# Second layer's gate and up projections from an h normalised ahead, in 512-column matmuls; first layer's feed-forward activations moved by 32 bytes

## The chip, the cores and the metric

The kernel runs on one core of one Trainium2 chip. The metric is the time of one execution in microseconds, as the median of several runs. The core has TensorE (matmuls, with a separate weight load), VectorE (DVE), ScalarE (ACT), GpSimd (POOL) and SyncE (SP), which here issues the DMAs of the weights. The engines run side by side and wait for each other by semaphores.

## What is computed

Two layers of a diffusion backbone over 512 latent tokens (`x`) and 256 context tokens (`ctx`), width 1024. Each layer has a mixing half (windowed attention and a convolution group, one output projection) and a feed-forward half. The change is in the latter:

```python
D_MODEL = 1024; SEQ = 512; CTX_LEN = 256; DEPTH = 2; D_FF = 2816
def rmsnorm(x, g):
    y = xf * lax.rsqrt(jnp.mean(xf * xf, axis=-1, keepdims=True) + EPS)
    return y * g
def modulate(h, shift, scale):
    return h * (1 + scale) + shift
def swiglu(h, w_gu, w_dn):
    gu = h @ w_gu
    return (jax.nn.silu(gu[..., :D_FF]) * gu[..., D_FF:]) @ w_dn
...
h2 = modulate(rmsnorm(x, g_ffn[l]), sh2, sc2)
x = x + gt2 * swiglu(h2, w_gate_up[l], w_down[l])
if not last:      # the same for the context tokens, with their own shift, scale and gate
    ...
return rmsnorm(x, g_final)
```

In the second layer (index 1) no context token goes through the feed-forward half.

## The kernel before

Features lie on the 128 partitions, tokens along the free axis: `x` is [128, 8, 768], eight feature tiles of 512 latent and 256 context tokens. All weights are float32. To keep float32 accuracy each operand is split into a high part (rounded to float32r) and a low part (the rest), and a product is three matmuls: high x high, low x high, high x low (`tile_product`, L488; the matmul is L496). A weight block is 128 output features by eight k-tiles of 128 rows: SyncE loads it into `raw0` or `raw1` (L397), ScalarE writes `w_high` (`split_high`, L736) and VectorE `w_low` (`split_low`, L1015). Two blocks make a pair, one for each of the two slots: weights, PSUM banks (slot 0 has banks 0 and 1, slot 1 has 2 and 3) and `tmp` are double. ScalarE starts the copy for the next use of a slot when the block on it has ended, so its starts mark the ends of blocks.

The modulated norm is not applied before the matmul. What TensorE reads as `h_high` and `h_low` (`hH`, `hL`) is x times gain only. 1/rms is per token and is multiplied in afterwards, and the shift goes through the weights as two further columns (one for latent, one for context tokens), kept behind the tokens in the same rows: 512 + 2 + 256 + 2 columns, 3088 bytes. So a block's columns come in two groups, `mod_cols` (L281): with context 512 and 258, without it 256 and 258, since a bank holds 512 columns. Each group is a matmul of its own:

```python
def mod_cols(context):
    return [(0, 0, N), (1, HC, HW)] if context else [(0, 0, N // 2), (1, N // 2, HC)]
```

The feed-forward half goes in three chunks of 8, 8 and 6 tiles of D_FF: `gu0`, `dn0`, `gu1`, `dn1`, `gu2`, `dn2`. A gate/up phase has one pair for each tile of D_FF: slot 0 is the gate, slot 1 the up half. For each (`gu_pair`), VectorE copies the two shift columns (L1059) and multiplies the product by 1/rms into `tmp` (L1060), which frees the PSUM slot; ScalarE takes Silu of the gate with the shift as bias (L958); VectorE adds the shift to the up half and multiplies (L1385); ScalarE writes `ff_high` (`aH`, L964), VectorE `ff_low` (`aL`, L1389). VectorE handles all this in the written order: scaling of slot 0, `w_low` of slot 0, scaling of slot 1, `w_low` of slot 1, product, `ff_low`. The down phase has four pairs (eight tiles of x); its k-tiles are the chunk's tiles of D_FF, with one matmul of 512 columns and, in layer 0, one of 256. TensorE waits for `ff_low` tile by tile.

1/rms of layer 1's feed-forward norm (`rs`) is ready only while TensorE is in pair 0 of `gu0`, as its sums go over TensorE in between (`stat_tokens`, `stat_broadcast`).

In layer 0 VectorE also sums the modulation vectors of layer 1 (`ada_multiply`) between feed-forward blocks.

Places in SBUF are worked out by nested scopes; tiles of different stages share bytes. `ff_high` starts at a multiple of 128 bytes, its rows are 3072 bytes.

Of the kernel before, what the change touches and what calls it, by code (L numbers as in the profile page):

```python
# [27 lines left out]
P = 128  # L28
# [63 lines left out]


def key_columns(tokens, tiles):


    if tiles == (0, 1, 4, 5):
        return tokens.rearrange("p (a c) -> p a c", c=2 * P)[:, 0:3:2, :]
    step = tiles[1] - tiles[0]
    if step == 1:  # L100
        return tokens[:, P * tiles[0]:P * (tiles[-1] + 1)]
    return tokens.rearrange("p (t c) -> p t c", c=P)[:, tiles[0]:tiles[-1] + 1:step, :]
# [22 lines left out]
def hybrid_backbone(nc, xT, params, w_ada, w_conv, w_mix, w_out, w_gu, w_dn0, w_dn1, w_dn2,  # L125
                    rope, ident_in, masks_in, out):
    with ExitStack() as ctx:
        def sb(name, shape, dt=F32):
            return ctx.enter_context(nc.sbuf_tensor(name, shape, dt))

        def sem(name):
            return ctx.enter_context(nc.semaphore(name))
# [4 lines left out]
        wH = [sb(f"w_high{j}", [P, DT, P], F32R) for j in range(2)]  # L137
        wL = [sb(f"w_low{j}", [P, DT, P], F32R) for j in range(2)]
        ada_raw = sb("ada_raw", [P, AGW])
        wD = sb("w_conv", [P, 2, TG, P])  # L140
# [38 lines left out]
        with ExitStack() as h_scope:  # L179
# [22 lines left out]
            with ExitStack() as s:  # L202
                s.enter_context(nc.sbuf_tensor("gap_ff", [P, 2 * max(CHUNKS) * T], F32))
                ada_in_ff = s.enter_context(nc.sbuf_tensor("ada_in_ff", [P, AGW], F32))
            with ExitStack() as s:
                aH = s.enter_context(nc.sbuf_tensor("ff_high", [P, max(CHUNKS), T], F32R))
                aL = s.enter_context(nc.sbuf_tensor("ff_low", [P, max(CHUNKS), T], F32R))
        with ExitStack() as s:
            prob = s.enter_context(nc.sbuf_tensor("prob", [P, 3, 5 * P], F32))
            V = s.enter_context(nc.sbuf_tensor("v_tokens", [P, TB, KV * HD], F32))  # L210

            s.enter_context(nc.sbuf_tensor("gap", [P, CT * HW - 5 * P * 3 - TB * KV * HD], F32))
            aT = s.enter_context(nc.sbuf_tensor("attn_out", [P, CT, T], F32))
            s.enter_context(nc.sbuf_tensor("gap2", [P, CT * (HW - T)], F32))
            PT = s.enter_context(nc.sbuf_tensor("probT", [P, 2, 5, GRP, P], F32))
# [48 lines left out]
        ff_high, ff_low = sem("ff_high_ready"), sem("ff_low_ready")  # L264
        y_ok = sem("out_tile_ready")
        dve_self, pool_self = sem("dve_self"), sem("pool_self")

# [5 lines left out]
        def streams(context):  # L273
            return [(0, N, 0)] + ([(N, T, 1)] if context else [])
# [18 lines left out]
        def gains(layer, which, context, k):  # L293
            return [(a, b, gain[:, layer, which, k, v:v + 1]) for a, b, v in streams(context)]

        def shift_cols(slot):
# [127 lines left out]
        def _(pe):  # L424
# [86 lines left out]
            def conv_tile(layer, k):  # L511
# [16 lines left out]
                last.then_inc(conv_mm, 1)  # L528

            def phase(layer, name, ktiles, rhsH, rhsL, cols, ready=None, key=None, blocks=TB):  # L530

# [158 lines left out]
            for layer in range(DEPTH):  # L690
# [26 lines left out]
                for c, tiles in enumerate(CHUNKS):  # L717
                    phase(layer, f"gu{c}", DT, hH, hL, mod_cols(context), (h_ok, h_index[layer, "n2"]) if c == 0 else None,
                          (layer, "n2") if c == 0 else None, blocks)
                    phase(layer, f"dn{c}", tiles, aH, aL, tok_cols(context, False), (ff_low, layer * FT + sum(CHUNKS[:c])))  # L720
            stat_tokens((DEPTH, "n1"), NB)
# [4 lines left out]
        def _(act):  # L726
# [141 lines left out]
            for layer in range(DEPTH):  # L868
# [81 lines left out]
                for c, tiles in enumerate(CHUNKS):  # L950
# [3 lines left out]
                    def gu_pair(i, first=False):  # L954
# [8 lines left out]
                        act.wait_ge(ff_ok, i + (ff + 1))  # L963
                        f(aH[:, i, 0:width], tmp[1][:, 0:width], ACT.Copy).then_inc(ff_high, 1)  # L964

                    gu_pair(0, first=True)
                    with act.Fori(1, tiles - 1) as i:
                        gu_pair(i)
                    gu_pair(tiles - 1)

# [33 lines left out]
        def _(dve):  # L1004
# [246 lines left out]
            for layer in range(DEPTH):  # L1251
# [116 lines left out]
                for c, tiles in enumerate(CHUNKS):  # L1368
                    gu, dn = f"gu{c}", f"dn{c}"
                    ff = layer * FT + sum(CHUNKS[:c])  # L1370

                    def gu_pair(i):
                        dve.wait_ge(gemm, i * 2 + (2 * USES[layer, gu] + 1))
                        scale_product(0, context)
                        split_low(layer, gu, i, 0)
                        if isinstance(i, int):
                            for u in ada_units(layer, gu, 2 * i):
                                ada_multiply(u)
# [9 lines left out]
                        dve.wait_ge(ff_high, i + (ff + 1))  # L1388
                        tt(aL[:, i, 0:width], tmp[1][:, 0:width], f32(aH[:, i, 0:width]), ALU.subtract).then_inc(ff_low, 1)  # L1389
                        dve.wait_ge(ff_low, i + (ff + 1))  # L1390

                    apart = tiles - 1 if (layer, gu) in ADA_IN else 1
                    for i in range(apart):
                        gu_pair(i)
                        if i == 0 and (layer, gu) in SUM_IN:
                            ada_columns(SUM_IN[layer, gu])
                    if apart < tiles - 1:
                        with dve.Fori(apart, tiles - 1) as i:
                            gu_pair(i)
                    gu_pair(tiles - 1)  # L1400

# [224 lines left out]
```

## Time and profile before

| | |
|---|---|
| median of 3 runs | 1590.11 us (1589.21 to 1590.46) |
| profiled execution, its own time | 1588.25 us |
| its span | 1586.4 us |
| TensorE busy | 1533.7 us (97%), 9714 matmuls |
| VectorE busy | 936.5 us (59%) |
| ScalarE busy | 536.9 us (34%) |
| chain that ended last | TensorE 86%, VectorE 6%, ScalarE 4% |
| granted TensorE clock, mean | 0.99 of 2.4 GHz |

The span runs from the first to the last recorded instruction. In timelines each row has a start and a length in microseconds from the span's start, engine, line of the kernel, operation, and in brackets the idle time before it with what ended it. A matmul's length holds its passage through the array, which overlaps the next, so the pace of matmuls is read from start to start. The chain is followed back from the last instruction.

### The profile page before, as it was taken

Reading aid. Unit: us, or ns where it says so; the run is one execution under the profiler, and the core shown is the slowest. Engines: PE = TensorE matmul, PEld = TensorE weight load, DVE = VectorE, ACT = ScalarE, POOL = GpSimd, SP = SyncE. Lnnn points to the kernel's source line nnn. Section 1 sums busy time; section 2 is a strip of 40 time slices with the busy share of each in tenths; the row PEclk is TensorE's granted clock in tenths of the full one; section 3 lists DMA queues with packets and bytes.
Section 4 is the critical chain, followed back from the end, with each engine's and each line's share of the span. In section 5 each row is a group of like instructions: output and inputs, shape, how many; then the busy total and the mean of one; then the engine's idle time right before and its main releaser. Section 6 shows DMA issues by size and latency. Waiting matters only on the chain.

```text
span 1586.4 us, 24584 instructions
## 1 busy us (share of the span) xinstructions
PE 1533.7 (97%) x9714; PEld 1274.5 (80%) x9714; DVE 936.5 (59%) x1571; ACT 536.9 (34%) x858; POOL 128.4 (8%) x163
## 2 busy tenths in 40 slices
PE   6999998999999999999999999998999999999996
PEld 3865764688888888888888888676679998998995
DVE  2584689767666325765654466678786443443445
ACT  3312378724222112221122243148844222322222
POOL 0033221040000000000000001511020000000000
PEclk9999999999999999999999999999999999999998
DMA  9582600012333223333522123410022332323222
GB/s 358 207 242 58 241 12 27 1 54 107 119 122 103 67 81 144 119 115 123 191 74 62 54 70 108 137 54 1 28 67 93 93 93 93 93 93 95 93 87 83
DMA packets 39865, 161.16 MB, mean 102 GB/s; under 512 B 5616, under 2 KB 6000, under 8 KB 33648
## 3 DMA queue, kind: packets, MB, share of 16 engines
q1 hardware_dynamic: 35856, 148.72, 27.6%
q0 software_dynamic: 3936, 11.45, 2.6%
q8 instruction: 47, 0.77, 0.2%
q14 instruction: 26, 0.21, 0.0%
HBM read 149.76 MB, written 2.10 MB: 96 GB/s over the span
## 4 chain that ended last, share of the span: by engine, by line
PE 86%; DVE 6%; ACT 4%; issue 2%; POOL 1%; DMA 1%; SPq 0%; DVEq 0%; ACTq 0%; POOLq 0%
PE banks L496 74%; PE banks L525 3%; PE banks L613 2%; PE banks L433 1%; PE banks L640 1%; PE banks L625 1%; POOL z_padded L1528 1%; DVE row_max L1132 1%; PE banks L677 1%; PE banks L465 1%; ACT prob L819 1%; PE banks L483 1%; ACT w_high L736 1%; DMA ada_first<-in_w_ada 1%; ACT probT L831 1%
## 5 line engine op out<-in xcount | busy, mean ns | idle before, releaser
L496 PE MATMUL banks<-h_high,w_high 128*128 128x512 f32 (+1 forms) x1856 | 433.0, 314 | 3.9 <-DVE w_low L1015 2.4
L496 PE MATMUL banks<-h_high,w_low 128*128 128x512 f32 (+1 forms) x1856 | 427.8, 312 | 0.0
L496 PE MATMUL banks<-h_low,w_high 128*128 128x512 f32 (+1 forms) x1856 | 426.5, 311 | 0.0
L736 ACT ACTIVATE w_high<-raw 128x1024 fp32r<-128x1024 f32 (+1 forms) x178 | 185.3, 1041 | 697.0 <-PE banks L496 677.7
L496 PEld LDWEIGHTS banks<-h_high,w_high 128*128 128x128 f32 x1856 | 288.0, 189 | 38.3 <-issue 14.6
L1015 DVE TENSOR_TENSOR w_low<-raw,w_high 128x1024 fp32r<-128x1024 f32 (+1 forms) x178 | 216.3, 1215 | 171.1 <-ACT w_high L736 167.5
L496 PEld LDWEIGHTS banks<-h_low,w_high 128*128 128x128 f32 x1856 | 287.7, 189 | 21.1
L496 PEld LDWEIGHTS banks<-h_high,w_low 128*128 128x128 f32 x1856 | 286.4, 189 | 20.6
L1059 DVE COPY shift_product<-banks 128x2 f32<-128x2 f32 x116 | 18.4, 159 | 310.1 <-PE banks L496 299.2
L496 PE MATMUL banks<-ff_high,w_high 128*128 128x512 f32 (+1 forms) x528 | 160.5, 358 | 0.6 <-DVE ff_low L1389 0.6
L496 PE MATMUL banks<-ff_high,w_low 128*128 128x512 f32 (+1 forms) x528 | 159.6, 357 | 0.0
L496 PE MATMUL banks<-ff_low,w_high 128*128 128x512 f32 (+1 forms) x528 | 159.0, 355 | 0.0
L496 PEld LDWEIGHTS banks<-ff_high,w_high 128*128 128x128 f32 x528 | 87.1, 188 | 17.5 <-issue 1.7
L496 PEld LDWEIGHTS banks<-ff_low,w_high 128*128 128x128 f32 x528 | 87.1, 188 | 15.4
L496 PEld LDWEIGHTS banks<-ff_high,w_low 128*128 128x128 f32 x528 | 86.6, 188 | 14.9
L1060 DVE TENSOR_TENSOR tmp<-banks,inv_root 128x768 f32<-128x768 f32 (+1 forms) x116 | 94.9, 819 | 0.0
L1132 DVE TENSOR_REDUCE row_max<-banks 128x1 f32<-128x512 f32 (+2 forms) x80 | 55.0, 688 | 19.6 <-PE banks L613 19.1
L1108 DVE SCALAR_TENSOR_TENSOR x<-banks,mod,x 128x512 f32<-128x512 f32 (+1 forms) x96 | 60.3, 656 | 10.5 <-PE banks L496 10.5
L964 ACT ACTIVATE ff_high<-tmp 128x768 f32 (+3 forms) x44 | 32.5, 740 | 97.3 <-DVE tmp L1385 97.3
L613 PE MATMUL banks<-k_stacked,q_stacked 128*128 128x384 f32 (+2 forms) x224 | 59.2, 369 | 5.4 <-ACT esink L821 2.9
L1389 DVE TENSOR_TENSOR ff_low<-tmp,ff_high 128x768 fp32r<-128x768 f32 (+3 forms) x44 | 36.3, 825 | 41.0 <-ACT ff_high L964 41.0
L1271 DVE SCALAR_TENSOR_TENSOR conv<-z_padded,par,conv 128x512 f32<-128x512 f32 x90 | 57.0, 660 | 2.0
(171 smaller groups left out, 1623.5 us busy)
## 6 DMA issues: line engine op xcount, KB each, us to landing
raw<-in_w_gu SPq DMA_DIRECT2D x88, 512.0 KB, 3.5
ada_raw<-in_w_ada SPq DMA_DIRECT2D x21, 1024.0 KB, 5.7
raw<-in_w_dn SPq DMA_DIRECT2D x32, 512.0 KB, 3.5
raw<-in_w_mix SPq DMA_DIRECT2D x28, 512.0 KB, 5.0
ada_in_ff<-in_w_ada SPq DMA_DIRECT2D x12, 1024.0 KB, 5.5
raw<-in_w_out SPq DMA_DIRECT2D x16, 512.0 KB, 3.5
ada_first<-in_w_ada SPq DMA_DIRECT2D x7, 1024.0 KB, 14.1
raw<-in_w_dn SPq DMA_DIRECT2D x16, 384.0 KB, 3.0
```

The source lines that it names most:

```text
L496: last = mm(bank[:, 2 * slot + bk, 0:b - a], weights[w][:, k0_w + k, :], rhs[:, k0_rhs + k, a:b], start=(k == 0 and n == 0), stop=(k == kt ...
L525: last = mm(bank[QC * q:QC * q + QC, BC + bk, 0:b - a], wD[:, j, g, QC * q:QC * q + QC], zr[j][:, q, SH * g + a:SH * g + b], start=(g == 0 ...
L613: last = mm(wide[:, at:at + w], lhs, rhs, start=in_bank[m] not in in_bank[:m], stop=in_bank[m] not in in_bank[m + 1:], skip_group_check=True)
L736: f(wH[j][:, 0:k, :], raw[j][:, 0:k, :], ACT.Copy).then_inc(w_high, 1)
L964: f(aH[:, i, 0:width], tmp[1][:, 0:width], ACT.Copy).then_inc(ff_high, 1)
L1015: tt(wL[j][:, 0:k, :], raw[j][:, 0:k, :], f32(wH[j][:, 0:k, :]), ALU.subtract).then_inc(w_low, 1)
L1059: nc.vector.tensor_copy(shifted[:, slot, :], shift_cols(slot))
L1060: tt(like(tmp[slot]), src, like(rs), ALU.mult).then_inc(slot_free[slot], 1)
L1108: last = stt(out=xt, in0=bank[:, 2 * slot + (a >= N), 0:b - a], scalar=mod[:, layer, bass.ds(t + gate * DT, 1), v], in1=xt, op0=ALU.mult, ...
L1132: nc.vector.reduce_max(mx[:, c:c + 1], score_place(u, qs[q][2]), AX.X).then_inc(row_ok, 1)
L1271: made = stt(out=acc, in0=zt, scalar=col("w_dw", j, layer), in1=acc, op0=ALU.mult, op1=ALU.add)
L1389: tt(aL[:, i, 0:width], tmp[1][:, 0:width], f32(aH[:, i, 0:width]), ALU.subtract).then_inc(ff_low, 1)
```

## The change

Layer 0's gate/up is computed as before. In layer 1, pairs 0 to 2 of chunk 0 are too (`PLAIN = 3`). Meanwhile VectorE multiplies x by gain and 1/rms (`h_normal`, a ring of six tiles), ScalarE adds the shift and rounds (`h_normal_high`), and VectorE writes the rest (`h_normal_low`): three tiles after pair 0, three after pair 1, two after pair 2, the low parts of a group following inside the next pair, those of the last two after pair 2. From pair 3 of chunk 0 on, and in chunks 1 and 2, TensorE reads these with one matmul of 512 columns for each product; Silu and the product read PSUM directly. Layer 1's activations get tiles of their own with rows of 512 tokens (`lastH`, `lastL`); layer 0's start 32 bytes further (`gap_line`).

```diff
...
+PLAIN = 3
+HN_RING = 6
...
+        with ExitStack() as s:
+            hn_high = s.enter_context(nc.sbuf_tensor("h_normal_high", [P, DT, N], F32R))
...
-                s.enter_context(nc.sbuf_tensor("gap_ff", [P, 2 * max(CHUNKS) * T], F32))
+                s.enter_context(nc.sbuf_tensor("gap_ff", [P, 2 * max(CHUNKS) * T + 16], F32))
+                s.enter_context(nc.sbuf_tensor("gap_line", [P, 8], F32))
+            with ExitStack() as s:
+                lastH = s.enter_context(nc.sbuf_tensor("ff_last_high", [P, max(CHUNKS), N], F32R))
+                lastL = s.enter_context(nc.sbuf_tensor("ff_last_low", [P, max(CHUNKS), N], F32R))
+                hn_low = s.enter_context(nc.sbuf_tensor("h_normal_low", [P, DT, N], F32R))
+                hn = s.enter_context(nc.sbuf_tensor("h_normal", [P, HN_RING, N], F32))
+            ffH, ffL = (aH, lastH), (aL, lastL)
...
+        hn_scaled, hn_hi, hn_ok = sem("h_normal_product"), sem("h_normal_high_ready"), sem("h_normal_ready")
...
+        def normal_from(layer, c):
+            return DT if layer == 0 else PLAIN if c == 0 else 0
...
+            def last_gu(c):
+                layer, name = 1, f"gu{c}"
+                key = (layer, "n2")
+                plain = normal_from(layer, c)
+                for i in range(plain):
+                    for j in range(2):
+                        after = [(7, lambda: stat_tokens(key, NB))] if i + j == 0 else \
+                            [(2, lambda: stat_broadcast(key, NB))] if i == 0 else ()
+                        gemm_block(layer, name, i, j, DT, hH, hL, mod_cols(False),
+                                   (h_ok, h_index[key]) if i + j == 0 else None, after)
+                for j in range(2):
+                    gemm_block(layer, name, plain, j, DT, hn_high, hn_low, [(0, 0, N)],
+                               (hn_ok, 0) if plain and j == 0 else None)
+                with pe.Fori(plain + 1, PAIRS_OF[name]) as i:
+                    for j in range(2):
+                        gemm_block(layer, name, i, j, DT, hn_high, hn_low, [(0, 0, N)])
...
-                    phase(layer, f"gu{c}", DT, hH, hL, mod_cols(context), (h_ok, h_index[layer, "n2"]) if c == 0 else None,
-                          (layer, "n2") if c == 0 else None, blocks)
-                    phase(layer, f"dn{c}", tiles, aH, aL, tok_cols(context, False), (ff_low, layer * FT + sum(CHUNKS[:c])))
+                    if layer:
+                        last_gu(c)
+                    else:
+                        phase(layer, f"gu{c}", DT, hH, hL, mod_cols(context), (h_ok, h_index[layer, "n2"]) if c == 0 else None,
+                              (layer, "n2") if c == 0 else None, blocks)
+                    phase(layer, f"dn{c}", tiles, ffH[layer], ffL[layer], tok_cols(context, False),
+                          (ff_low, layer * FT + sum(CHUNKS[:c])))
...
-                        f(aH[:, i, 0:width], tmp[1][:, 0:width], ACT.Copy).then_inc(ff_high, 1)
-                    gu_pair(0, first=True)
-                    with act.Fori(1, tiles - 1) as i:
-                        gu_pair(i)
-                    gu_pair(tiles - 1)
+                        f(ffH[layer][:, i, 0:width], tmp[1][:, 0:width], ACT.Copy).then_inc(ff_high, 1)
+                    def normal_high(first, last):
+                        for k in range(first, last):
+                            act.wait_ge(hn_scaled, k + 1)
+                            f(hn_high[:, k, :], hn[:, k % HN_RING, :], ACT.Identity,
+                              bias=mod[:, layer, 3 * DT + k, 0:1]).then_inc(hn_hi, 1)
+                    def gu_normal(i):
+                        split_high(layer, gu, i, 0)
+                        f(act_out[:, 0:N], bank[:, 0, 0:N], ACT.Silu).then_inc(slot_free[0], 1)
+                        split_high(layer, gu, i, 1)
+                        act.wait_ge(slot_free[1], i + (USES[layer, gu] + 1))
+                        f(ffH[layer][:, i, 0:N], tmp[1][:, 0:N], ACT.Copy).then_inc(ff_high, 1)
+                    if layer == 0:
+                        gu_pair(0, first=True)
+                        with act.Fori(1, tiles - 1) as i:
+                            gu_pair(i)
+                        gu_pair(tiles - 1)
+                    else:
+                        plain = normal_from(layer, c)
+                        for i in range(plain):
+                            gu_pair(i)
+                            normal_high(*((0, 3), (3, 6), (6, 8))[i])
+                        with act.Fori(plain, tiles - 1) as i:
+                            gu_normal(i)
+                        gu_normal(tiles - 1)
...
-                    def gu_pair(i):
+                    def gu_pair(i, between=None):
+                        if between is not None:
+                            between()
...
-                        tt(aL[:, i, 0:width], tmp[1][:, 0:width], f32(aH[:, i, 0:width]), ALU.subtract).then_inc(ff_low, 1)
+                        tt(ffL[layer][:, i, 0:width], tmp[1][:, 0:width], f32(ffH[layer][:, i, 0:width]), ALU.subtract)\
+                            .then_inc(ff_low, 1)
-                    apart = tiles - 1 if (layer, gu) in ADA_IN else 1
+                    def normal_product(first, last):
+                        for k in range(first, last):
+                            if k >= HN_RING:
+                                dve.wait_ge(hn_ok, k - HN_RING + 1)
+                            stt(out=hn[:, k % HN_RING, :], in0=x[:, k, 0:N], scalar=gain[:, layer, 1, k, 0:1],
+                                in1=rs[:, 0:N], op0=ALU.mult, op1=ALU.mult).then_inc(hn_scaled, 1)
+                    def normal_low(first, last):
+                        for k in range(first, last):
+                            dve.wait_ge(hn_hi, k + 1)
+                            stt(out=hn_low[:, k, :], in0=hn[:, k % HN_RING, :], scalar=mod[:, layer, 3 * DT + k, 0:1],
+                                in1=f32(hn_high[:, k, :]), op0=ALU.add, op1=ALU.subtract).then_inc(hn_ok, 1)
+                    def gu_normal(i):
+                        split_low(layer, gu, i, 0)
+                        dve.wait_ge(gemm, i * 2 + (2 * USES[layer, gu] + 2))
+                        dve.wait_ge(slot_free[0], i + (USES[layer, gu] + 1))
+                        tt(tmp[1][:, 0:N], bank[:, 2, 0:N], act_out[:, 0:N], ALU.mult).then_inc(slot_free[1], 1)
+                        split_low(layer, gu, i, 1)
+                        dve.wait_ge(ff_high, i + (ff + 1))
+                        tt(ffL[layer][:, i, 0:N], tmp[1][:, 0:N], f32(ffH[layer][:, i, 0:N]), ALU.subtract).then_inc(ff_low, 1)
+                        dve.wait_ge(ff_low, i + (ff + 1))
+                    if layer:
+                        plain = normal_from(layer, c)
+                        for i in range(plain):
+                            gu_pair(i, (lambda: normal_low(0, 3), lambda: normal_low(3, 6))[i - 1] if i else None)
+                            normal_product(*((0, 3), (3, 6), (6, 8))[i])
+                        if plain:
+                            normal_low(6, 8)
+                        with dve.Fori(plain, tiles - 1) as i:
+                            gu_normal(i)
+                        gu_normal(tiles - 1)
+                    apart = 0 if layer else tiles - 1 if (layer, gu) in ADA_IN else 1
-                    if apart < tiles - 1:
+                    if layer == 0 and apart < tiles - 1:
-                    gu_pair(tiles - 1)
+                    if layer == 0:
+                        gu_pair(tiles - 1)
```

## Rows read from the trace of the kernel before

**Rows 1.** The page: busy time with share and instructions of each engine.
```profile
PE 1533.7 (97%) x9714; PEld 1274.5 (80%) x9714; DVE 936.5 (59%) x1571; ACT 536.9 (34%) x858; POOL 128.4 (8%) x163
```

**Rows 2.** The chain that ended last: start us, length us, piece.
```profile
1206.74 330.36 PE banks L496 x2430
1541.07 29.55 PE banks L496 x129
```

**Rows 3.** Groups by line and form, 1207 to 1537 us: count, busy us, mean ns.
```profile
L496 PE MATMUL banks<-h_high,w_high 128*128 128x258 f32 x340 | 95.4, 281 | 0.0
L496 PE MATMUL banks<-ff_high,w_high 128*128 128x512 f32 x129 | 50.2, 389 | 0.0
```

**Rows 4.** Timeline of ScalarE, gate/up of layer 1: start us, length us, instruction, idle before.
```profile
1221.76 1.06 ACT L736 ACTIVATE w_high<-raw 128x1024 fp32r<-128x1024 f32 x1 [3.95 <-PE banks L496]
1233.17 1.06 ACT L736 ACTIVATE w_high<-raw 128x1024 fp32r<-128x1024 f32 x1 [3.95 <-PE banks L496]
```

**Rows 5.** Timeline, down projection of chunk 0, layer 1, ScalarE.
```profile
1295.70 1.06 ACT L736 ACTIVATE w_high<-raw 128x1024 fp32r<-128x1024 f32 x1 [1.81 <-PE banks L496]
1301.14 1.06 ACT L736 ACTIVATE w_high<-raw 128x1024 fp32r<-128x1024 f32 x1 [4.38 <-PE banks L496]
```

**Rows 6.** Timeline at the start of the last down projection.
```profile
1537.13 0.84 ACT L736 ACTIVATE w_high<-raw 128x768 fp32r<-128x768 f32 x1 [4.19 <-PE banks L496]
1540.10 0.39 PE L496 MATMUL banks<-ff_high,w_low 128*128 128x512 f32 x1
1540.33 0.69 DVE L1389 TENSOR_TENSOR ff_low<-tmp,ff_high 128x512 fp32r<-128x512 f32 x1 [0.70 <-ACT ff_high L964]
1541.07 0.50 PE L496 MATMUL banks<-ff_high,w_high 128*128 128x512 f32 x1 [0.58 <-DVE ff_low L1389]
```

**Rows 7.** Timelines of layer 1: VectorE, two subtractions, then pairs 1 and 2; last ScalarE.
```profile
1200.00 1.41 DVE L1045 SCALAR_TENSOR_TENSOR h_low<-x,gain,h_high 128x512 fp32r<-128x512 f32 x2
1227.47 0.16 DVE L1059 COPY shift_product<-banks 128x2 f32<-128x2 f32 x1 [1.11 <-PE banks L496]
1228.65 1.23 DVE L1015 TENSOR_TENSOR w_low<-raw,w_high 128x1024 fp32r<-128x1024 f32 x1 [0.42 <-ACT w_high L736]
1233.18 0.16 DVE L1059 COPY shift_product<-banks 128x2 f32<-128x2 f32 x1 [3.30 <-PE banks L496]
1235.41 0.74 DVE L1385 SCALAR_TENSOR_TENSOR tmp<-tmp,shift_product,act_out 128x512 f32<-128x512 f32 x1
1237.08 0.69 DVE L1389 TENSOR_TENSOR ff_low<-tmp,ff_high 128x512 f32 x1 [0.92 <-ACT ff_high L964]
1236.29 0.63 ACT L964 ACTIVATE ff_high<-tmp 128x512 f32 x1 [2.05 <-DVE tmp L1385]
```

**Rows 8.** Timeline of ScalarE in layer 0: gate/up, then down projection of chunk 1.
```profile
591.22 1.06 ACT L736 ACTIVATE w_high<-raw 128x1024 fp32r<-128x1024 f32 x1 [7.42 <-PE banks L496]
...
624.91 1.06 ACT L736 ACTIVATE w_high<-raw 128x1024 fp32r<-128x1024 f32 x1 [6.16 <-PE banks L496]
...
745.39 1.06 ACT L736 ACTIVATE w_high<-raw 128x1024 fp32r<-128x1024 f32 x1 [6.36 <-PE banks L496]
...
779.32 1.06 ACT L736 ACTIVATE w_high<-raw 128x1024 fp32r<-128x1024 f32 x1 [7.33 <-PE banks L496]
```

**Rows 9.** Timeline of TensorE: matmuls after two gaps.
```profile
969.58 0.58 PE L496 MATMUL banks<-h_high,w_high 128*128 128x256 f32 x1 [2.40 <-DVE w_low L1015]
...
1094.44 0.77 PE L625 MATMUL banks<-ident,prob 128*128 128x128 f32 x5 [1.84 <-DVE prob L1155]
```

**Rows 10.** Busy time by stretch: each engine, then granted clock, DMA share, GB/s.
```profile
969.30:972.70 3.40, 3.12 (x14) 3.12 (x15) 2.77 (x5) 1.93 (x2) 0.00 (x0) 0.51 0.41 152
...
1095.60:1099.00 3.40, 3.40 (x15) 2.33 (x14) 2.96 (x8) 2.69 (x6) 0.00 (x0) 0.50 0.00 0
```

**Rows 11.** Timeline of TensorE at half clock.
```profile
970.17 0.63 PE L496 MATMUL banks<-h_low,w_high 128*128 128x256 f32 x2
970.60 0.63 PE L496 MATMUL banks<-h_high,w_low 128*128 128x256 f32 x2
```

## The prediction

> **What bounds the kernel now.** I read the page's busy times first, then the chain that ended last, then timelines of the feed-forward part of layer 1. TensorE is busy 97% of the span [rows 1]. The chain of waits says the same of the place that changes: from 1206.74 us on it stays on the product line L496 for 330 us without a break, and again from 1541.07 for 29.55 us [rows 2]. So in this stretch a shorter stream of matmuls shortens the run one for one, and work of VectorE or ScalarE counts only where it makes TensorE wait.
>
> The reader should see how the stream differs between the two kinds of phase. In gate/up of layer 1 every weight tile meets the tokens in two matmuls, one of 256 and one of 258 columns; down projections of the same layer use one of 512 [rows 3]. The durations in these rows (281 and 389 ns) include the drain and overlap, so they don't price a matmul; the pace of whole blocks does. ScalarE starts its weight copy when a block ends. In gate/up two blocks, 96 matmuls, lie between 1221.76 and 1233.17: 11.41 us, 118.9 ns each, so a pair (512 tokens and the two shift columns) costs 237.7 ns [rows 4]. In the down projection one block of 24 lies between 1295.70 and 1301.14: 5.44 us, 226.7 ns each [rows 5]. Over the array time at 2.4 GHz both carry 12 to 13 ns; the wide form carries it once.
>
> **Part 1, wide matmuls.** Pairs 0 to 2 of chunk 0 stay as they are. The blocks that change are 2 x (5 + 8 + 6) = 38, with 24 products each: 912 pairs become 912 single matmuls. 912 x (237.7 - 226.7) = 10.0 us, all on TensorE's path. The new operands are read as ff_high and ff_low are in [rows 5]: 512 columns, one bank, rows a multiple of 1024 bytes apart, starts a multiple of 128 bytes. The price could be another, since high and low now come from two regions. The lower bound is 226.7. For the upper one I take layer 0: there a block of 24 pairs of 512 and 256 or 258 columns takes (624.91 - 591.22)/4 = 8.42 us in gate/up and (779.32 - 745.39)/4 = 8.48 us in the down projection [rows 8]; 350.9 and 353.4 ns a pair, less 118.9 for the narrow one, leave 232.0 and 234.5 for the wide. I take 226.7, as the down rows are the only ones with the same form alone; the ends are 10.0 and 2.9 us.
>
> By the Trainium skill ("TensorE: Matmul & The Clock Gate", section "Back-to-back issue gap") a warm matmul takes its columns at 2.4 GHz plus a fixed 2.5 ns. By that rule joining two would give only 2.5 ns and the two shift columns (0.8 ns), 3.0 us for 912, an estimate from that page, and the whole change would come out level. The rows above stand against it: both forms carry about five times that fixed part.
>
> **Part 2, the end of a gate/up pair.** From pair 3 on the shift is already in h: ScalarE takes Silu straight from PSUM, VectorE multiplies straight from PSUM, and the copy L1059, the scaling L1060 of both halves and the product L1385 shrink to one operation. Mostly this is hidden, as VectorE is far from full. It shows once: at the start of the last down projection, which needs the last activation tile after five k-steps (3.4 us). There the weight copy starts at 1537.13, ff_low starts at 1540.33 and TensorE resumes at 1541.07, having started its last matmul at 1540.10, where 0.23 us is the pace: 0.74 us lost [rows 6]. With the shorter tail: product 0.7 beside the weight copy 0.84, ff_high 0.63, then w_low 0.96 and ff_low 0.69, so about 1537.13 + 2.6 = 1539.7, before 1540.33 when the tile is wanted. The 0.7 us go. Before the other two chunks there is no such wait (eight k-steps, 4.8 us), so nothing is gained. Next late there is nothing: the weights for that block are a block ahead.
>
> **Part 3, making h ahead.** Added are 8 products and 8 subtractions on VectorE and 8 copies on ScalarE, all of 512 columns. Their like in the trace: 0.75 us for L1385 (0.67 apiece where two stand in a row, 1.41 us for both), 0.63 for L964 [rows 7]. That is 10.7 us of VectorE and 5 of ScalarE, put between the work of three pairs that last 11.4 us each. I follow the queues. Queued behind the three products of a pair are the next pair's scaling, which frees a PSUM slot, and behind ScalarE's three copies its next weight copy. Pair 2's first scaling stands at 1227.47 now; behind products 3 to 5 (pair 1's ff_low ends about 1226.4, plus 3 x 0.67) it comes at 1228.5. ScalarE's weight copy comes at 1229.2, w_low at 1230.4 to 1231.6, wanted at 1233.0 for block 6: 1.4 us to spare, no wait. Then the subtractions 3 to 5 until 1233.6, scaling of slot 1 (now 1233.18) until 1234.4, its w_low until 1235.5, product, ff_high, ff_low until about 1237.7 (now 1237.08 + 0.69, so it hardly moves). Only after that come products 6 and 7 (1237.7 to 1239.1), ScalarE's copies (1238.5 to 1239.8), and subtractions 6 and 7, which end at 1239.9 and 1240.6.
>
> Block 6 is the first that reads the new h. It starts at 1233.0 and reaches k = 6 after six steps of 3 x 0.2267 us, at 1237.05. It waits for tile 6 until 1239.9 and hardly for tile 7: a new stall of 2.9 us, once. Bounds: 1.5 if the VectorE work slips in earlier than I place it, 4.5 if each handover costs 0.3 us more.
>
> **What the stall does to the clock.** In this trace TensorE's gaps of 2.40 and 1.84 us are followed by a stretch at granted clock 0.5, the lower level of 1.2 GHz [rows 9, 10]. The three others of over 1.8 us have such a stretch behind them too; the gaps of 1.01 us and less have none. In the half-clock stretch pairs of 256 and 258 columns start 0.427 us apart (970.17, 970.60) instead of 0.238 [rows 11]. A stretch of 3.4 us therefore does 1.9 us of work: 1.5 us lost. I add 1.5; the bounds are 0 and 3.
>
> **Part 4, the shift of layer 0's activations by 32 bytes.** It adds no instruction. It can only change how fast TensorE reads ff_high and ff_low in the first layer's down projections, 22 k-steps by 8 blocks by 3 = 528 pairs. They run at 8.48 us a block while gate/up of the same layer, whose rows start at staggered offsets, runs at 8.42 [rows 8]: 2.5 ns a pair. If the shift only breaks a bad standing relation, the down projections come to the gate/up figure: 528 x 2.5 ns = 1.3 us. Some of it falls in chunk 1, after which VectorE's sums set the pace for a while, so I count 0.9. Bounds: 4.1 us gained if the pair falls to 226.7 + 118.9 = 345.6, and as much lost the other way.
>
> **Sum**, against the profiled execution (span 1586.4, its own time 1588.25): -10.0 - 0.7 + 2.9 + 1.5 - 0.9 = -7.2 us, so 1581.0. The median of the runs shown, 1590.11, is 1.9 us above the profiled execution, and I forecast a median: 1582.9.
>
> **Rivals.** (a) The stream in the second layer doesn't reach the down projection's pace but keeps the 232.0 ns of layer 0's wide matmuls. For it: the high and low parts lie in different regions; against it: the layer 0 figure comes with a narrow matmul in between. Then part 1 gives 5.2 us instead of 10.0 and the time is 1587.7, within the noise. If joining two matmuls saves almost nothing but the two columns, as the 234.5 ns of layer 0's down projections would have it, part 1 gives 2.9 us and the time is 1590.0. I give 0.14 to the stream at 232 and 0.02 to that at 234.5. (The rule of the Trainium skill, "TensorE: Matmul & The Clock Gate", above leads to the same 234.5 ns.)
> (b) The stall isn't there or leaves the clock alone. Without the clock loss 1581.4, without the stall too 1578.5. For it: my schedule is from starts of other operations; against it: the products 6 and 7 stand behind pair 2's ff_low in VectorE's order. 0.13.
> (c) Layer 0 gains the full 4.1 us: 1579.7. For it: nothing but that 345.6 is what the two forms cost alone. 0.08.
> (d) Slower: the down projections of layer 0 lose by the shift. The reads of both operands no longer start at a multiple of 64 bytes; no row shows such a start for ff. The rest of the change is worth 6.3 us, so it decides from 6.3/528 = 12 ns a pair; at 20 ns the time is 1590.1 - 6.3 + 10.6 = 1594.4. Against it: layer 0's h rows start at every 16 bytes and their pairs are the faster ones. 0.04.
> (e) That it doesn't do what it says: blocks from pair 3 on would still issue 48 matmuls. The code excludes it; no chance given.
>
> **How the numbers follow.** The forecast has 0.59, (a) 0.16, (b) 0.13, (c) 0.08, (d) 0.04. The likeliest gives 1582.9. The range has to take in most of (a), (b) and (c): 1578.6 to 1587.6; left out are (d), the far side of (a), and the case that (b) and (c) meet. About 0.2% (3.2 us) is what a measurement of this kernel can tell from no change. Faster by more than that: the forecast, (b), (c) and a third of (a), 0.86. Within it: the rest of (a) and a bit of (d), 0.11. Slower: 0.03.
>
> **What would show it.** Right: weight copies of ScalarE 5.44 us apart in gate/up of layer 1 from pair 3 on; one gap on TensorE of about 3 us inside the seventh block of chunk 0, ended by h_normal_low, with a stretch at half clock behind it; no gap before the last down projection; layer 0's down blocks at 8.42. Wrong: a spacing of 5.57 us (232 ns each) means (a); no gap means my order of VectorE's queue was wrong; down blocks of layer 0 above 8.48 mean that the shift works against the kernel, and above 8.77 it decides the sign.

## The result and the profile after

The changed kernel takes 1577.82 us (median of 4, 1576.94 to 1579.26) against 1589.66 us (median of 4, 1587.55 to 1590.46): ratio 0.9932, 95% interval 0.9919 to 0.9944, so 10.8 us less (8.9 to 12.9). A second series gave 0.9936 (0.9924 to 0.9949). Forecast were 7.2 us less and a range from 1578.6; the sign was right, the gain too small by 3.6 us, and the median lies 0.8 us below the range. (The range was counted from a before of 1590.11, which is 0.45 above this series' 1589.66; 0.9932 x 1590.11 = 1579.3 lies inside it.)

The page of the changed kernel, as [rows 1], and its chain of waits, as [rows 2]; line numbers have moved (the product line L496 is L514 now):

```profile
span 1577.4 us, 22649 instructions
PE 1519.3 (96%) x8802; PEld 1229.0 (78%) x8802; DVE 919.2 (58%) x1511; ACT 537.1 (34%) x866; POOL 128.6 (8%) x163
```

```profile
1204.61 26.41 PE banks L514 x222
1231.04 1.07 ACT w_high L776
1232.17 1.11 issue
1237.79 324.26 PE banks L514 x1422
```

912 matmuls fewer, the number in the forecast. From 1237.79 us on the chain stays on the products for 324 us: the wait before the last down projection [rows 6] is gone. Where the time went, by ScalarE's weight copies at the same blocks (us from the start of the span):

| point | before | after | difference |
|---|---|---|---|
| layer 0, start of its first down projection | 520.89 | 520.98 | +0.1 |
| layer 0, end of block 5 (of 8) of its second | 779.32 | 777.17 | -2.2 |
| layer 1, first weight wait | 967.2 | 964.4 | -2.8 |
| layer 1, end of block 1 of `gu0` | 1210.35 | 1208.21 | -2.1 |
| end of `gu0` | 1290.24 | 1290.08 | -0.2 |
| end of `gu1` | 1425.10 | 1420.63 | -4.5 |
| end of `gu2` | 1537.13 | 1529.43 | -7.7 |
| last weight copy | 1562.48 | 1553.91 | -8.6 |
| end of span | 1586.4 | 1577.4 | -9.0 |

Read downwards: layer 0 gives 2.8, of which 0.7 go in the attention of layer 1, untouched by the change (last section), `gu0` takes 2.0 back, `gu1` gives 4.3 and `gu2` 3.2, the last down projection 0.9 and the rest 0.4. (The execution profiled after the change is the slowest of its four, so the spans differ by less than the medians.)

Blocks of gate/up in layer 1, chunk 0, timeline of ScalarE, as [rows 4]: two blocks in 10.89 us instead of 11.41.

```profile
1257.43 1.06 ACT L776 ACTIVATE w_high<-raw 128x1024 fp32r<-128x1024 f32 x1 [3.81 <-PE banks L514]
...
1268.32 1.06 ACT L776 ACTIVATE w_high<-raw 128x1024 fp32r<-128x1024 f32 x1 [3.81 <-PE banks L514]
```

The new stall, timelines of TensorE and VectorE in block 6; compare the order with [rows 7]: `ff_low` first, then the products of tiles 6 and 7 (L1463), then their low parts (L1469), on whose first TensorE waits.

```profile
1234.70 0.39 PE L514 MATMUL banks<-h_normal_high,w_low 128*128 128x512 f32 x1
1237.79 0.50 PE L514 MATMUL banks<-h_normal_high,w_high 128*128 128x512 f32 x1 [2.71 <-DVE h_normal_low L1469]
```

```profile
1234.72 0.69 DVE L1454 TENSOR_TENSOR ff_last_low<-tmp,ff_last_high 128x512 fp32r<-128x512 f32 x1 [0.70 <-ACT ff_last_high L1004]
1235.45 1.42 DVE L1463 SCALAR_TENSOR_TENSOR h_normal<-x,gain,inv_root 128x512 f32<-128x512 f32 x2
1236.99 1.42 DVE L1469 SCALAR_TENSOR_TENSOR h_normal_low<-h_normal,mod,h_normal_high 128x512 fp32r<-128x512 f32 x2
```

Behind it the granted clock falls to 0.50 for 3.4 us (busy times, then clock, as [rows 10]), and matmuls of 512 columns start 0.43 us apart:

```profile
1238.92:1242.34 3.42, 3.42 (x10) 2.65 (x9) 1.23 (x1) 1.54 (x2) 0.00 (x0) 0.50 0.00 0
```

```profile
1240.02 0.63 PE L514 MATMUL banks<-h_normal_low,w_high 128*128 128x512 f32 x1
1240.45 0.63 PE L514 MATMUL banks<-h_normal_high,w_low 128*128 128x512 f32 x1
```

Start of the last down projection, ScalarE and VectorE, as [rows 6]: `ff_low` starts 1.76 us behind the block's end instead of 3.20, and the first block takes 4.08 us instead of 4.94.

```profile
1529.43 0.85 ACT L776 ACTIVATE w_high<-raw 128x768 fp32r<-128x768 f32 x1 [4.11 <-PE banks L514]
1530.19 0.61 ACT L1018 ACTIVATE ff_last_high<-tmp 128x512 fp32r<-128x512 f32 x1
1533.51 0.85 ACT L776 ACTIVATE w_high<-raw 128x768 fp32r<-128x768 f32 x1 [2.71 <-PE banks L514]
```

```profile
1529.43 0.69 DVE L1477 TENSOR_TENSOR tmp<-banks,act_out 128x512 f32<-128x512 f32 x1 [3.60 <-PE banks L514]
1530.32 0.96 DVE L1078 TENSOR_TENSOR w_low<-raw,w_high 128x768 fp32r<-128x768 f32 x1 [0.19 <-ACT w_high L776]
1531.19 0.69 DVE L1480 TENSOR_TENSOR ff_last_low<-tmp,ff_last_high 128x512 fp32r<-128x512 f32 x1
```

Down projection of layer 0, chunk 1, ScalarE, as the last two of [rows 8]: four blocks in 33.28 us, 8.32 each, where there were 8.48. This is the term that the forecast had too small.

```profile
743.89 1.06 ACT L776 ACTIVATE w_high<-raw 128x1024 fp32r<-128x1024 f32 x1 [6.26 <-PE banks L514]
...
777.17 1.06 ACT L776 ACTIVATE w_high<-raw 128x1024 fp32r<-128x1024 f32 x1 [7.18 <-PE banks L514]
```

### The profile page after: what moved, and what is told of

It reads as the page before. It is cut to its first block, busy times and chain, and to the rows that moved or that the text cites. A ratio compares the mean times of both kernels' runs of the same rounds, so it can differ in the third digit from the quotient of the medians.

```text
span 1577.4 us, 22649 instructions
## 1 busy us (share of the span) xinstructions
PE 1519.3 (96%) x8802; PEld 1229.0 (78%) x8802; DVE 919.2 (58%) x1511; ACT 537.1 (34%) x866; POOL 128.6 (8%) x163
## 4 chain that ended last, share of the span: by engine, by line
PE 86%; DVE 6%; ACT 4%; issue 2%; POOL 1%; DMA 1%; SPq 0%; DVEq 0%; ACTq 0%; POOLq 0%
PE banks L514 74%; PE banks L543 3%; PE banks L649 2%; PE banks L451 1%; PE banks L676 1%; PE banks L661 1%; DVE row_max L1195 1%; PE banks L713 1%; ACT prob L859 1%; PE banks L483 1%; PE banks L501 1%; POOL z_padded L1630 1%; DMA ada_first<-in_w_ada 1%; ACT probT L871 1%; ACT w_high L776 0%
## 5 line engine op out<-in xcount | busy, mean ns | idle before, releaser
L514 PE MATMUL banks<-h_high,w_high 128*128 128x512 f32 (+1 forms) x1248 | 310.8, 330 | 4.6 <-DVE w_low L1078 2.4
L514 PE MATMUL banks<-h_high,w_low 128*128 128x512 f32 (+1 forms) x1248 | 304.8, 325 | 0.0
L514 PE MATMUL banks<-h_low,w_high 128*128 128x512 f32 (+1 forms) x1248 | 304.0, 325 | 0.0
L514 PEld LDWEIGHTS banks<-h_high,w_high 128*128 128x128 f32 x1248 | 193.3, 189 | 38.6 <-issue 15.2
L514 PEld LDWEIGHTS banks<-h_low,w_high 128*128 128x128 f32 x1248 | 193.5, 189 | 20.9
L514 PEld LDWEIGHTS banks<-h_high,w_low 128*128 128x128 f32 x1248 | 192.0, 189 | 20.4
L514 PE MATMUL banks<-h_normal_high,w_high 128*128 128x512 f32 x304 | 119.1, 392 | 2.7 <-DVE h_normal_low L1469 2.7
L514 PE MATMUL banks<-h_normal_high,w_low 128*128 128x512 f32 x304 | 119.1, 392 | 0.0
L514 PE MATMUL banks<-h_normal_low,w_high 128*128 128x512 f32 x304 | 119.0, 392 | 0.0
L514 PE MATMUL banks<-ff_high,w_high 128*128 128x512 f32 x352 | 90.2, 337 | 0.0
L514 PE MATMUL banks<-ff_low,w_high 128*128 128x512 f32 x352 | 89.9, 336 | 0.0
L514 PE MATMUL banks<-ff_high,w_low 128*128 128x512 f32 x352 | 89.9, 336 | 0.0
L514 PEld LDWEIGHTS banks<-h_normal_high,w_high 128*128 128x128 f32 x304 | 57.5, 189 | 15.1 <-DVE h_normal_low L1469 3.1
L514 PE MATMUL banks<-ff_last_high,w_high 128*128 128x512 f32 x176 | 68.5, 389 | 0.0
L514 PE MATMUL banks<-ff_last_low,w_high 128*128 128x512 f32 x176 | 68.5, 389 | 0.0
L514 PE MATMUL banks<-ff_last_high,w_low 128*128 128x512 f32 x176 | 68.5, 389 | 0.0
```

What stands on the lines that cost most here:

```text
L514: last = mm(bank[:, 2 * slot + bk, 0:b - a], weights[w][:, k0_w + k, :], rhs[:, k0_rhs + k, a:b], start=(k == 0 and n == 0), stop=(k == kt ...
```

## The experiments

### The shift alone

```diff
+                s.enter_context(nc.sbuf_tensor("gap_line", [P, 8], F32))     # kernel before, gap_ff 16 longer
                 aH = s.enter_context(nc.sbuf_tensor("ff_high", [P, max(CHUNKS), T], F32R))
```

> The kernel before with one edit: layer 0's feed-forward activations (ff_high, ff_low) start 32 bytes further. My forecast had 0.9 us for this part; the changed kernel's profile shows the down blocks of layer 0 at 8.32 us instead of 8.48, which is 22 x 0.16 = 3.5 us if nothing hides it. Theory A (the shift acts alone, through TensorE's pace in these blocks): 2.0 to 3.5 us faster than before, down blocks at 8.32. Theory B (the pace comes from something else in the changed kernel, such as its different code): no change, blocks at 8.48.

Measured: 0.9994 of before (0.9985 to 1.0003), no difference that can be told, where theory A expected 2.0 to 3.5 us. Yet layer 0's down blocks are at 8.32, as theory A has it. The other half is in layer 1, whose activations were shifted too here, as both layers share the tiles. Timeline of ScalarE, two pieces: four down blocks of layer 0, and the last block of `dn0` in layer 1 (all eight take 44.79 us, 5.60 each, and so do those of `dn1`):

```profile
743.53 1.06 ACT L737 ACTIVATE w_high<-raw 128x1024 fp32r<-128x1024 f32 x1 [6.26 <-PE banks L497]
...
776.81 1.06 ACT L737 ACTIVATE w_high<-raw 128x1024 fp32r<-128x1024 f32 x1 [7.18 <-PE banks L497]
```

```profile
1326.15 1.06 ACT L737 ACTIVATE w_high<-raw 128x1024 fp32r<-128x1024 f32 x1 [4.54 <-PE banks L497]
1331.75 1.06 ACT L737 ACTIVATE w_high<-raw 128x1024 fp32r<-128x1024 f32 x1 [4.54 <-PE banks L497]
```

Layer 1's down blocks, one matmul of 512 columns per product, have gone from 5.44 us [rows 5] to 5.60, 233.3 ns a matmul instead of 226.7. Layer 0 gives 3.3 us (the end of block 1 of `gu0` at 1207.06 instead of 1210.35), layer 1 takes back 2 x 1.25 in its first two down projections and 0.8 in the last, so that the stream of products ends at 1570.66 instead of 1570.62. So the same offset helps the stream of alternating 512 and 256 columns and harms the stream of 512 alone. In the changed kernel only layer 0's tiles move; layer 1's have their own at the old place, and that half of the edit counts as much as the shift.

### The changed kernel without the shift

```diff
-                s.enter_context(nc.sbuf_tensor("gap_line", [P, 8], F32))     # changed kernel
```

> The changed kernel with layer 0's activations back at their old place. Theory A: down blocks of layer 0 at 8.48 again, and 2.0 to 3.5 us slower than the changed kernel, so 7.5 to 9 us faster than before, all of it from layer 1. Theory B: as fast as the changed kernel.

Measured: 0.9958 of before (0.9944 to 0.9971), 6.7 us less, where the changed kernel has 10.8 less; layer 0's down blocks back at 8.48:

```profile
747.50 1.06 ACT L775 ACTIVATE w_high<-raw 128x1024 fp32r<-128x1024 f32 x1 [6.36 <-PE banks L513]
...
781.42 1.06 ACT L775 ACTIVATE w_high<-raw 128x1024 fp32r<-128x1024 f32 x1 [7.34 <-PE banks L513]
```

The intervals of the two ratios just touch (0.9944), and the second series of the changed kernel (0.9936, up to 0.9949) overlaps a little; the block times leave no doubt of the direction. Theory A holds: 3.5 to 4 us of the change are the shift by the ratios (22 blocks x 0.16 allow 3.5), some 7 the rest, a little less than the 7.5 expected.

### Weights moved instead, and everything moved

```diff
+        sb("gap_w0", [P, 8])                                              # kernel before
         wH = [sb(f"w_high{j}", [P, DT, P], F32R) for j in range(2)]
         wL = [sb(f"w_low{j}", [P, DT, P], F32R) for j in range(2)]
+        sb("gap_w1", [P, 8])
```

> The kernel before with w_high and w_low 32 bytes further and all activations where they stand to a 64-byte line. Theory A1 (what counts is where the moving rows lie against the weights): layer 0's down blocks go to 8.32 us as in the changed kernel. Theory A2 (what counts is where the moving rows lie by themselves): they stay at 8.48. The gate/up blocks of layer 0 (8.42) are looked at too.

Measured in a single execution, whose block times are read and not its total, as with the next three: layer 0's down blocks 8.32, layer 1's 5.60 - the figures of the first experiment, though the activations have moved by 64 bytes and so still start at a multiple of 64. Gate/up of layer 0 takes 8.43 (8.42 before).

```profile
1324.87 1.06 ACT L738 ACTIVATE w_high<-raw 128x1024 fp32r<-128x1024 f32 x1 [4.54 <-PE banks L498]
1330.47 1.06 ACT L738 ACTIVATE w_high<-raw 128x1024 fp32r<-128x1024 f32 x1 [4.54 <-PE banks L498]
```

One thing stayed possible: that either operand off its line is enough. So both were moved, by leaving out the second gap:

> The kernel before with w_high and everything behind it in SBUF 32 bytes further, weights and moving rows alike, so their distance is as before while no start lies on a 64-byte line any more. Theory A1 (the distance between moving rows and weights sets the pace): 8.48 us a down block in layer 0 and 5.44 in layer 1, as before. Theory A2 (either start off its line does it, which the runs with one of them moved can't exclude): 8.32 and 5.60.

```profile
1329.35 1.06 ACT L737 ACTIVATE w_high<-raw 128x1024 fp32r<-128x1024 f32 x1 [4.38 <-PE banks L497]
1334.79 1.06 ACT L737 ACTIVATE w_high<-raw 128x1024 fp32r<-128x1024 f32 x1 [4.38 <-PE banks L497]
```

Layer 1 at 5.44 and layer 0 at 8.48, as before. Theory A1 holds for these 32 bytes: what counts is the distance in SBUF between the moving rows and the weights, not where either lies. That the distance isn't all that sets the pace shows further down (rows of h).

### Other distances

The kernel before with a gap of 16 floats, and with both tiles as slices of one, 4 floats in:

> The kernel before with ff_high and ff_low of both layers 64 bytes further. If the 64-byte line counts: 8.48 us a down block in layer 0 and 5.44 in layer 1, as before. If a longer line counts (128 bytes): other figures, up to 8.32 and 5.60 as at 32 bytes.

> The kernel before with ff_high and ff_low of both layers 16 bytes further (slices of one tile). If any start off the line costs the same: 8.32 us a down block in layer 0 and 5.60 in layer 1, as at 32 bytes. If it goes by the distance: in between.

Block times in us, both layers' activations moved:

| distance to the weights, against before | layer 0 (512 and 256 columns) | layer 1 (512) |
|---|---|---|
| 0 (before, and all moved by 32) | 8.48 | 5.44 |
| +16 bytes | 8.32 | 5.56 |
| +32 bytes (activations up, or weights) | 8.32 | 5.60 |
| +64 bytes | 8.48 | 5.49 |

At 64 bytes layer 0 is back where it was and layer 1 isn't. So neither "the 64-byte line" nor one longer line is the whole rule.

### Rows of h at the same kind of offset

```diff
+HROW = 784                                       # beside HW = 772; the rest as in the four-pair version (below)
...
+        sb("gap_before_h", [P, 8])
...
-            hH = h_scope.enter_context(nc.sbuf_tensor("h_high", [P, DT, HW], F32R))
-            hL = h_scope.enter_context(nc.sbuf_tensor("h_low", [P, DT, HW], F32R))
+            hH = h_scope.enter_context(nc.sbuf_tensor("h_high", [P, DT, HROW], F32R))
+            hL = h_scope.enter_context(nc.sbuf_tensor("h_low", [P, DT, HROW], F32R))
+            h_scope.enter_context(nc.sbuf_tensor("gap_after_h", [P, 8], F32))
```

> The version with four narrow pairs, and in addition the rows of h_high and h_low 3136 bytes apart instead of 3088, starting 32 bytes past a 64-byte line as the weights don't; all else stays where it was to a line. Seen so far: streams that alternate 512 and 256 columns take 8.32 us a block with that offset and 8.48 without; gate/up of layer 0, with staggered rows, takes 8.42. Theory A (the offset of the moving rows against the weights sets the pace of such streams, whatever the tile): gate/up of layer 0 goes to about 8.33 a block, 44 blocks x 0.09 = 4.0 us, and the u and q/k/v blocks of layer 0 give another 1, so 4 to 5 us faster than the four-pair version and 7 to 9 faster than the changed kernel. Theory B (the effect belongs to the ff tiles or to the down projection's code): gate/up stays at 8.42 and the time is that of the four-pair version, 3.5 us faster than the changed kernel.

Theory A fell: 0.9970 of before (0.9958 to 0.9982), 8 to 10 us slower than the four-pair version. Layer 0's gate/up stays at (640.66 - 607.01)/4 = 8.41 us. And all that lies behind h moved by 832 bytes, a multiple of 64, which I had taken for harmless: layer 0's down blocks are at 8.40 and layer 1's wide gate/up blocks at 5.57 instead of 5.44. Of the latter's operands only `h_normal_low` moved against the weights:

```profile
1355.86 1.06 ACT L779 ACTIVATE w_high<-raw 128x1024 fp32r<-128x1024 f32 x1 [3.96 <-PE banks L517]
...
1366.98 1.06 ACT L779 ACTIVATE w_high<-raw 128x1024 fp32r<-128x1024 f32 x1 [3.94 <-PE banks L517]
```

Layer 1's down blocks are the surprise. Start and end of `dn0`, then of `dn1`:

```profile
1289.63 1.06 ACT L779 ACTIVATE w_high<-raw 128x1024 fp32r<-128x1024 f32 x1 [4.00 <-PE banks L517]
...
1333.59 1.06 ACT L779 ACTIVATE w_high<-raw 128x1024 fp32r<-128x1024 f32 x1 [4.43 <-PE banks L517]
...
1422.66 1.06 ACT L779 ACTIVATE w_high<-raw 128x1024 fp32r<-128x1024 f32 x1 [4.03 <-PE banks L517]
...
1467.46 1.06 ACT L779 ACTIVATE w_high<-raw 128x1024 fp32r<-128x1024 f32 x1 [4.54 <-PE banks L517]
```

Eight blocks take 43.96 us in `dn0` and 44.80 in `dn1`, 5.50 and 5.60 each, at a granted clock of 1.00 in both. Both phases read the same tiles at the same places, with the same weights' tiles. So something besides the distance sets the pace here, and no run shows what; where the phase's instructions lie is one candidate that was not tested. In every other run the two phases are alike.

22 x 0.08 + 36 x 0.13 + 8 x 0.06 + 8 x 0.16 + 0.3 = 8.5 us, which is about the loss. The rows of this h are 3136 bytes apart and those of the weights 512, so each k-step has another distance. Whether one good distance for all rows would bring gate/up to 8.32 was not tried.

### No stall: four narrow pairs, or tiles of h in fours

```diff
-PLAIN = 3                                                             # changed kernel
+PLAIN = 4                                     # and normal_low(6, 8) inside pair 3
```

> The changed kernel with four pairs of layer 1 as before instead of three, and the low parts of h tiles 6 and 7 made inside the fourth, so that all eight tiles are ready before the first block that reads them. Theory A (the stall of 2.7 us in the seventh block and the half-clock stretch behind it, 1.6 us, cost what they seem to): they go, two narrow blocks cost 0.27 us each, so 3.7 us faster than the changed kernel. Theory B (VectorE is the bound there, and the stall only moves to a wait for weights): at most 1 us faster.

Measured 1574.29 us, 0.9910 of before (0.9895 to 0.9925); in a second series beside the next version 1575.70, 0.9913 (0.9900 to 0.9927).

```diff
-                            normal_product(*((0, 3), (3, 6), (6, 8))[i])     # changed kernel, PLAIN = 3
+                            normal_product(*((0, 4), (4, 8), (8, 8))[i])     # low parts and copies alike
```

> The changed kernel with its three narrow pairs, but the tiles of h made in two groups of four (products 0 to 3 after pair 0, 4 to 7 after pair 1, low parts inside pairs 1 and 2), so that none is left for after pair 2. Theory A (the stall of 2.7 us in the seventh block comes only from products 6 and 7 standing behind pair 2's ff_low; weights for blocks 4 and 6 have over 1 us to spare): no gap on TensorE in gu0, no half-clock stretch there, 0.5 us faster than the version with four narrow pairs and 4 us faster than the changed kernel. Theory B (VectorE is full in these pairs): the wait moves to w_low of block 4 or 6, and the time is at most 2 us better than the changed kernel.

> The version with four narrow pairs once more, timed beside the last. About 3.7 us faster than the changed kernel, 14 us (0.9%) faster than the kernel before.

Measured 1575.02 us, 0.9908 of before (0.9893 to 0.9923). TensorE has no gap in this stretch in either, and the clock stays up. Busy times of the version in fours from the end of pair 0 (1211.56) through pairs 1 and 2 into pair 3: TensorE first (29.00 of 29.00), VectorE third (23.80), the clock after the five engines (1.00):

```profile
1211.00:1240.00 29.00, 29.00 (x223) 28.02 (x222) 23.80 (x37) 14.28 (x20) 0.00 (x0) 1.00 0.31 92
```

From the end of block 1 to the end of `gu0`: before 79.9 us, changed 81.9, four pairs 77.8, fours 77.2. Without the stall the change thus gains 2.1 to 2.7 us in chunk 0 where it lost 2.0. The 0.5 us between the last two are seen in the stretch and not in the medians. Both beat the changed kernel: 3 to 4.5 us by the ratios, 4.1 and 4.7 in the stretch; the intervals of the ratios overlap in part, so that the stretch carries this reading.

In the second series of the changed kernel the stretch at half clock behind the stall was twice as long, and the stretch took 83.1 us:

> The changed kernel once more, timed beside the next version on the same chip. About 11 us (0.7%) faster than the kernel before.

```profile
1236.40:1243.20 6.80, 6.12 (x14) 4.79 (x15) 2.52 (x3) 2.05 (x3) 0.00 (x0) 0.50 0.00 0
```

Measured 1579.67 us, 0.9936 of before.

## Why the forecast was right or wrong

**Wide matmuls, 10.0 us: right.** 16 blocks of `gu1` take 4.3 us less and 12 of `gu2` 3.2: 0.268 us a block, 10.2 for 38. Taking the down projection's 226.7 ns [rows 5] was the right choice over the 232.0 from layer 0. The reason I gave, rows and starts at multiples of 1024 and 128 bytes as in the down projection, points at the right thing, as with `h_normal_low` displaced the block takes 5.57. But it isn't the multiples: with weights and activations both 32 bytes further no start is at a multiple of 128, and the down block still takes 5.44.

**Shorter end of a pair, 0.7 us: right.** 0.86 by the first block of the last down projection. `ff_low` starts 1.44 us sooner behind the block.

**The stall, 2.9 us: right**, 2.71 by the profile, in the block and for the reason given; the two versions without it show that VectorE was not full. Products 6 and 7 start 4.4 us behind the end of block 5 (1231.04), forecast was 4.5.

**The clock, 1.5 us: right in this execution**, with 3.4 us at 0.50: blocks 6 and 7 take 4.64 us more than two others, 1.9 beyond the stall. But what the trace of before shows of every gap over 1.8 us is no rule. In the changed kernel's profile the gap of 2.40 us at 964.4 has no stretch at half clock, nor has the one of 1.82 us that ends at 1092.91, where the same gaps have one before [rows 9, 10]; the stretch behind the new stall was 3.4 us once and 6.8 once.

**The 32 bytes, 0.9 us: the term that was mis-sized.** The shift gives 2.8 us in layer 0 by the profiles, and 3.5 to 4 by the ratios of the kernels with and without it. I let the down projection come to the 8.42 us of gate/up, because "the shift only breaks a bad standing relation"; it goes to 8.32, as 346.7 ns a pair is nearly the two forms' own 345.6. Gate/up was no floor; its staggered rows may make it a mean over good and bad distances, which no run shows. That was rival (c), 4.1 us, to which I gave 0.08 because nothing spoke for it; the sum of the forecast's other terms with it is -10.4, and measured are -10.8. Of 22 x 0.16 = 3.5 us some 0.6 are missing at 964.4, where other engines set the pace for a while, as allowed for.

The two profiled executions add up: -10.2 (wide matmuls) - 0.9 (end of a pair) + 2.7 (stall) + 1.9 (clock) - 2.8 (shift) + 0.7 (attention of layer 1, not forecast) - 0.4 (behind the last product) = -9.0 us, the difference of the spans. Against -7.2 the shift alone makes 1.9 of it. What lies between -9.0 and the -10.8 of the medians is that the profiled execution was the slowest of its four; that the sum with rival (c) comes so near to -10.8 is in part luck.

**Rival (d)**, that the shift harms, holds for the other form: in layer 1 it costs 0.16 us a block. I had priced it for layer 0 alone and had not seen that leaving layer 1 out of the shift is worth 3.3 us.

**The other rivals.** (a) needed a stream at 232.0; it runs at 226.7. (b) needed an earlier place for products 6 and 7; there was none, though grouping the same operations in fours gives one.

## What to carry to other kernels

Join two matmuls of half the width where a bank allows it, and price it by the pace of whole blocks of either form in the same trace, not by the rows' durations. When a producer is made a stage ahead, follow the last of its tiles through the in-order queue: two tiles that stood behind a less urgent operation cost 4 to 5 us in the profiles of this stretch, and regrouping them gave that back. Before moving a tile in SBUF for any reason, look at what lies behind it: a displacement of some bytes against the weights moved block times by up to 3%, in opposite directions for two forms of the same stream.

## What was not expected of the hardware

The pace of a matmul stream depends on the distance in SBUF between its moving rows and its weights: 8.32 to 8.48 us for the same 48 matmuls, 5.44 to 5.60 for 24. The runs show that at 32 bytes it is the distance (all moved: no change), that 16 and 32 bytes are nearly alike, and that displacements of 64 and 832 bytes still matter. They also show that it isn't the distance alone: 5.50 and 5.60 us for the same operands at the same places in one execution. What in the machine does either they don't show.

The clock's stretches differ between executions of one kernel. In the changed kernel's profile a half-clock stretch at 1054.6 was 3.4 us long and was followed by a gap of 2.87 us and 6.8 us more at half clock; so it is in seven of the thirteen profiles; in the six where the first stretch was 6.8 us long, the kernel before among them, the later gap was under 1 us (and 3.4 us at half clock came later still, behind the gap of 1.8 us). Rows of TensorE, changed kernel:

```profile
1072.29 0.73 PE L649 MATMUL banks<-k_stacked,q_stacked 128*128 128x512 f32 x2 [1.04 <-DVE tmp L1123]
1075.97 1.22 PE L649 MATMUL banks<-k_stacked,q_stacked 128*128 128x512 f32 x2 [2.87 <-ACT esink L861]
```

This is a good part of the 2 to 4 us by which executions of one kernel spread. The version with four narrow pairs was profiled once of each kind: with the gap of 2.87 us its span is 1573.9 us, with one of 0.96 it is 1570.3, and 2.2 of these 3.6 us arise between 949 and 1205 us, where it lies. So 0.5 us had to be read from a stretch.
